# An fp32 transformer stack on one core: the attention mixer's value panels, the order of its head steps, and its output rows

## The chip, the cores and the metric
One Trainium2 chip, one of its cores. The metric is the device time of one execution in microseconds (us), as the median of several runs. Three runs of the kernel before are shown, and one more execution was profiled.

## The reference, cut to what matters
Six layers with 256 tokens and 1024 features run one after the other, all in fp32. Each layer is a feed-forward sublayer, a mixer and a second feed-forward sublayer, each behind an RMS norm and added to the stream. The mixers are HGRN, differential attention, pooling, HGRN again, a hybrid and a recurrent one. The change is in the differential attention (eight heads, each with two groups of 64 query and key features and one value of 128 features):

```python
def diff_attention(x, w_in, lam, subln_w, w_out, layer):
    ...
    q, k, v = jnp.split(x @ w_in, 3, axis=-1)
    ...
        s = jnp.einsum('bhgqd,bhgkd->bhgqk', qb, k).astype(f32) * scale
        s = s - slopes[None, :, None, None, None] * dist
        p = jax.nn.softmax(jnp.where(allowed, s, -jnp.inf), axis=-1)
        w = p[:, :, 0] - lam_full * p[:, :, 1]
        return jnp.einsum('bhqk,bhkv->bhqv', w.astype(v.dtype), v)
    ...
    o = rmsnorm(o, subln_w) * (1.0 - lam_init)
    return o.reshape(B, S, D_MODEL) @ w_out
```

## The kernel before, in words
Activations lie with features on partitions and the 256 tokens along the free axis. Weights come in panels of 1 MB (1024 rows by 256 columns, `[128, 2048]` in memory), one DMA each from the queue of SyncE, into five slots `raw`. A slot is loaded again once TensorE has done the product of the panel in it (`panel_done`). All panels of the program form one list, and each engine goes through it in order.

**Split panels.** An fp32 product is made of reduced-precision parts. ScalarE copies a panel to its high part `whi` (line 1555) and VectorE subtracts it to get the low part `wlo` (line 1747), four panels ahead of TensorE (`AHEAD`). The input `xs` holds a high and a low half for each of eight feature tiles. `tile_product` issues, for each tile, one matmul of `whi` with 512 columns (line 1980) and one of `wlo` with 256 (line 1981). ScalarE copies the second half of the sum out of PSUM (line 1645, `corr_copied`), VectorE adds it (line 1827, `panel_out`) and multiplies by the input's norm factor (line 1917).

**Whole panels.** Output projections of mixers (`out_rows`, `out_rest`, line 2130) and the value panels of the two HGRN mixers (`token_product`, line 2033) use the raw fp32 weights, without a split. A value panel has the input `y` as its stationary operand (written by `whole_input`, line 1572), so that the result has tokens on partitions; ScalarE alone reads it out (`read_tokens`, line 1579, `tokens_out`), scaled by a norm factor for each token, which needs two small sums (line 2104) and two small operations on ScalarE (lines 1565, 1567).

**The attention mixer** reads twelve panels in the order q0 k0 v0 q1 k1 v1 and so on; a panel holds two heads (a pair). All twelve are split panels. Work of the heads is put between them by the table `AT_DELAYS`: a step of pair j stands behind panel 3j + d on its engine, cut off at 12, so what is due later stands behind the last panel, one step after the other. The engines run these lists strictly in order. For each head: `scores` (line 565, TensorE), `max` (bias, maximum: lines 637, 642 and 645, VectorE), `exp` (line 606, ScalarE), `weights` (lines 650 to 659, VectorE), `turn` (transposes of the weights, line 574, TensorE), `wT` (line 611, ScalarE), `values` (lines 582 to 584, TensorE). For each pair: `turn_values` (line 556, TensorE; its copy out is line 599 on ScalarE), `out` (line 664), `square` (614), `sums` (587), `rstd` (618, 620) and `norm` (669). Only when the step behind panel 12 is over does TensorE begin the output projection: `out_products` takes all eight feature tiles of the mixer's output for the first two panels (lines 2164 and 2165), then `out_rest` the other two. The transposes share PSUM bank 2, values and sums bank 3, the scores banks 0 and 1.

The rows of q, k and weights are double-buffered by pair or by head (`at`). The projection's output panels may begin when the bank of the panel two before has been read (`out_begin`).

Of the kernel before, what the change touches and what calls it, by code (L numbers as in the profile page):

```python
# [12 lines left out]
ACT = mybir.ActivationFunctionType  # L13
AX_X = mybir.AxisListType.X
# [49 lines left out]
def build(nc, a, out):  # L64
# [9 lines left out]
    for l in range(4):  # L74
# [6 lines left out]
        elif l == 1:  # L81
            subs.append(dict(kind=DIFF, gain=g + 2, layer=l, segs=[Segment("diff_in", 3 * D // PC), out_proj("diff_out")]))
# [42 lines left out]
    with ctx:  # L125
# [379 lines left out]
        AT_SUM, AT_REC = 4, 8  # L505

        def at_slot(n):
            return mix[:, 2 + n // 4, 2 * (n % 4):2 * (n % 4) + 2, :]

        def at(name, j):  # L510

            names = ("q", "k", "vt", "w", "wT")
            return at_slot(2 * names.index(name) + j % 2 if name in names else 10 + ("v", "sq", "r").index(name))
# [10 lines left out]
        def at_panel(p):  # L524
            return "qkv"[p % 3], p // 3


        AT_DELAYS = dict(
            pe=(("scores0", 3), ("turn_values", 4), ("scores1", 4), ("turn0", 5), ("turn1", 6), ("values0", 6), ("values1", 7),
                ("sums", 8)),  # L530
            act=(("exp0", 3), ("values", 4), ("exp1", 4), ("wT0", 5), ("wT1", 6), ("square", 7), ("rstd", 8)),
            dve=(("max0", 3), ("weights0", 4), ("max1", 4), ("weights1", 5), ("out", 7), ("norm", 8)))

        def at_steps(engine, p, step):

            left = []
            for j in range(KD // 2):
                for name, d in AT_DELAYS[engine]:
                    if min(3 * j + d, 3 * KD // 2) == p:
                        left.append((3 * j + d, j, name))  # L540
            for _, j, name in sorted(left, key=lambda x: x[:2]):
                step(name, j)

        def pe_at_step(pe, s, groups):
            n0, dg, mm = 0, P // groups, nc.tensor.matmul

            def step(name, j):
                n = n0 + j + 1
                h = int(name[-1]) if name[-1] in "01" else 0
                m = 2 * (n - 1) + h + 1  # L550
                if name == "turn_values":
                    pe.wait_ge(sem("at_values_in"), n)
                    if j:
                        pe.wait_ge(sem("at_wT"), m - 1)
                    for c in range(4):
                        e = nc.tensor.transpose(pm[:, 2, c * P:(c + 1) * P], flat_pair(at("v", j))[:, c * P:(c + 1) * P], ident[:, :])
                    e.then_inc(sem("at_values_turned"), 1)
                elif name.startswith("scores"):
                    pe.wait_ge(sem("at_keys_in"), n)
                    if m > 1:  # L560
                        pe.wait_ge(sem("at_scores_read"), m - 1)
                    for g in range(groups):
# [5 lines left out]
                elif name.startswith("turn"):  # L568
                    pe.wait_ge(sem("at_weights"), m)
                    pe.wait_ge(sem("at_vt"), n if h == 0 else n)  # L570
                    if h:
                        pe.wait_ge(sem("at_wT"), m - 1)
# [3 lines left out]
                elif name.startswith("values"):  # L576
                    pe.wait_ge(sem("at_wT"), m)
                    if j and h == 0:
                        pe.wait_ge(sem("at_rstd"), n - 1)
# [139 lines left out]

# [1556 lines left out]
```

## Time and profile before

| | |
|---|---|
| median of three runs | 3265.2 us (3262.81 to 3276.85) |
| the profiled execution | 3276.81 us, of which the span of its instructions is 3275.1 us |
| mean granted TensorE clock | 0.983 of full speed |
| TensorE busy | 97% of the span |
| VectorE, ScalarE busy | 68%, 52% |
| attention mixer: third panel to the first output row | 753.4 to 865.6 us |
| attention mixer: output projection | 865.6 to 895.6 us |

Each row of the page or of the trace names a source line, an engine, an operation and what it writes and reads. Times are from the start of the span. In brackets stands the idle time of the engine ahead of a row, and what ended it. An end of a matmul is modelled: the next one starts before it, so that what a step costs is read from one start to the next. An fp32 matmul has two records.

### The profile page before, as it was taken

What the parts mean: (1) busy time and instruction counts of PE and PEld (TensorE: products, weight loads), DVE (VectorE), ACT (ScalarE), POOL (GpSimd) and SP (SyncE); (2) the same over time, 40 slices, a digit from 0 to 9 for tenths busy, and PEclk for the clock granted to TensorE, in tenths of its full rate; (3) what the DMA queues carried; (4) which work ended last, traced back from release to release, by engine and by line L of the source; (5) the groups of instructions that cost most, each with busy time, mean ns of one, the idle gap of its engine ahead of it and who ended that gap; (6) DMA issues with size and microseconds to landing.
All of it is one profiled execution on the core that took longest, in us unless ns stands there. A gap on an engine that the chain in (4) does not pass through costs nothing.

```text
span 3275.1 us, 44778 instructions
## 1 busy us (share of the span) xinstructions
PE 3162.5 (97%) x18060; PEld 2734.9 (84%) x18060; DVE 2238.2 (68%) x2722; ACT 1703.6 (52%) x2092; POOL 4.2 (0%) x21
## 2 busy tenths in 40 slices
PE   9999999999799999999999999999787999999998
PEld 7888888887688888888888888888675888888887
DVE  7666775757486776675858586775865675866674
ACT  6465555544364654554546554554342554545553
POOL 0000000000000000000000000000000000000000
PEclk9999999999899999999999999999996999999999
DMA  6543454553245454454554345454330455454353
GB/s 225 191 167 129 154 186 175 185 188 129 90 173 187 172 188 169 152 182 167 193 190 155 125 173 181 180 181 173 141 135 1 145 190 182 179 182 162 145 185 124
DMA packets 75357, 534.79 MB, mean 163 GB/s; under 512 B 8480, under 2 KB 8608, under 8 KB 10784
## 3 DMA queue, kind: packets, MB, share of 16 engines
q1 hardware_dynamic: 75168, 532.07, 45.5%
q8 instruction: 143, 2.34, 0.3%
q14 instruction: 46, 0.38, 0.0%
HBM read 530.99 MB, written 1.05 MB: 162 GB/s over the span
## 4 chain that ended last, share of the span: by engine, by line
PE 89%; DVE 5%; DVEq 2%; ACT 2%; issue 1%; SPq 0%; DMA 0%; ACTq 0%
PE pp L1980 36%; PE pp L1981 18%; PE pm L1980 8%; PE pp L2130 4%; PE pm L1981 4%; PE pp L2003 4%; PE pp L1975 2%; PE pp L1974 2%; PE pp L1976 2%; PE pp L2005 2%; PE pp L2033 2%; DVE wlo L1747 1%; DVEq L405 0%; PE pm L1007 0%; ACT whi L1555 0%
## 5 line engine op out<-in xcount | busy, mean ns | idle before, releaser
L1980 PE MATMUL pp<-xs,whi 128*128 128x512 f32 x4720 | 1681.6, 401 | 6.8 <-DVE tsum L1827 6.5
L1747 DVE TENSOR_TENSOR wlo<-raw,whi 128x2048 fp32r<-128x2048 f32 x469 | 1072.7, 2290 | 420.8 <-ACT whi L1555 420.1
L1981 PE MATMUL pp<-xs,wlo 128*128 128x256 f32 x4720 | 1326.3, 281 | 0.0
L1980 PEld LDWEIGHTS pp<-xs,whi 128*128 128x128 f32 x4720 | 888.4, 188 | 237.3 <-DVE tsum L1827 16.0
L1555 ACT ACTIVATE whi<-raw 128x2048 fp32r<-128x2048 f32 x469 | 894.7, 1911 | 291.5 <-DMA raw<-weights 290.8
L1981 PEld LDWEIGHTS pp<-xs,wlo 128*128 128x128 f32 x4720 | 893.3, 189 | 0.8 <-issue 0.2
L1645 ACT ACTIVATE corr<-pp 128x512 f32<-128x512 f32 x344 | 204.5, 595 | 638.8 <-PE pp L1981 613.7
L1827 DVE TENSOR_TENSOR tsum<-pp,corr 128x512 f32<-128x512 f32 x331 | 228.5, 690 | 277.1 <-ACT corr L1645 276.6
L1980 PE MATMUL pm<-hs,whi 128*128 128x512 f32 x1120 | 400.2, 397 | 0.0
L1981 PE MATMUL pm<-hs,wlo 128*128 128x256 f32 x1120 | 314.7, 281 | 0.0
L1980 PEld LDWEIGHTS pm<-hs,whi 128*128 128x128 f32 x1120 | 210.9, 188 | 47.8
L1981 PEld LDWEIGHTS pm<-hs,wlo 128*128 128x128 f32 x1120 | 210.2, 188 | 0.0
L1980 PE MATMUL pp<-hs,whi 128*128 128x512 f32 x560 | 202.3, 397 | 0.0
L2003 PE MATMUL pp<-xs,whi 128*128 128x512 f32 x576 | 166.2, 400 | 16.2 <-DVE xs L1758 16.2
L1974 PE MATMUL pp<-hs,whi 128*128 128x256 f32 x560 | 159.7, 285 | 0.0
L1976 PE MATMUL pp<-hs,wlo 128*128 128x256 f32 x560 | 157.4, 281 | 0.0
L1981 PE MATMUL pp<-hs,wlo 128*128 128x256 f32 x560 | 157.4, 281 | 0.0
L1975 PE MATMUL pp<-hs,whi 128*128 128x256 f32 x560 | 157.4, 281 | 0.0
L1657 ACT ACTIVATE hs<-hid 128x512 fp32r<-128x512 f32 x132 | 83.7, 634 | 105.9 <-DVE hid L1843 105.9
L1980 PEld LDWEIGHTS pp<-hs,whi 128*128 128x128 f32 x560 | 105.3, 188 | 26.0
L2003 PEld LDWEIGHTS pp<-xs,whi 128*128 128x128 f32 x576 | 95.5, 188 | 33.6 <-issue 22.5
L2130 PE MATMUL pp<-mix,raw 128*128 128x256 f32 x512 | 115.2, 386 | 2.5 <-DVE mix L356 2.5
(355 smaller groups left out, 3072.6 us busy)
## 6 DMA issues: line engine op xcount, KB each, us to landing
raw<-weights SPq DMA_DIRECT2D x503, 1024.0 KB, 4.8
raw<-weights SPq DMA_DIRECT2D x8, 256.0 KB, 6.2
h<-x_by_feature SPq DMA_DIRECT2D x4, 256.0 KB, 6.7
out<-h SPq DMA_DIRECT2D x4, 256.0 KB, 2.5
vec<-vectors SPq DMA_DIRECT2D x1, 264.0 KB, 2.7
lamrow<-diff_lambda SPq DMA_DIRECT2D x1, 128.0 KB, 10.8
skiprow<-ssm_d SPq DMA_DIRECT2D x1, 8.0 KB, 11.4
```

The source lines that it names most:

```text
L1555: nc.scalar.activation(whi[:, slot, :], raw[:, slot, :], ACT.Copy).then_inc(sem("weights_hi"), 1)
L1645: nc.scalar.activation(two(corr[:, half, :]), banks[:, :, T:2 * T], ACT.Copy).then_inc(sem("corr_copied"), 1)
L1657: nc.scalar.activation(hs[:, 2 * j:2 * j + 2, 0:T], two(hid[:, :]), ACT.Copy).then_inc(sem("hidden_hi"), 1)
L1747: v.tensor_tensor(wlo[:, slot, :], raw[:, slot, :], whi[:, slot, :].bitcast(F32), ALU.subtract).then_inc(sem("weights_lo"), 1)
L1827: v.tensor_tensor(to, banks[:, :, 0:T], two(corr[:, half, :]), ALU.add).then_inc(sem("panel_out"), 1)
L1974: mm(bank[:, 0:T], whi[:, slot, c:c + P], x_k[:, 0:T], start=start, stop=False)
L1975: mm(bank[:, 0:T], whi[:, slot, c:c + P], x_k[:, T:2 * T], start=False, stop=False)
L1976: return mm(bank[:, 0:T], wlo[:, slot, c:c + P], x_k[:, 0:T], start=False, stop=stop)
L1980: mm(bank, whi[:, slot, c:c + P], x_k, start=start, stop=False)
L1981: return mm(bank[:, 0:T], wlo[:, slot, c:c + P], x_k[:, 0:T], start=False, stop=stop)
L2003: e = mm(bank, whi[:, slot, c:c + P], xs[:, k, :], start=(k == 0), stop=(k == KD - 1))
L2130: return mm(in_banks[p % 2][:, ft, 0:T], raw[:, g % SLOTS, c:c + P], x[:, k, :], start=start, stop=stop)
```

## The change
The four value panels of the attention mixer become whole fp32 panels with tokens on partitions, as in HGRN. With that, `turn_values` (TensorE), its copy (ScalarE), and the splits and reads of these four panels go, and the mixer takes `whole_input` and the sums for each token. The panels come in a new order, q0 k0 q1 k1 v0 q2 k2 q3 k3 v1 v2 v3. A table written out by hand (`AT_PLAN`) says which step of which head stands behind which panel on each engine: every head's `scores`, `turn` and `values` are about one panel behind the previous head's. Of the value and `wT` tiles there are four buffers now. `sums` of pairs 1 to 3 go to the banks of the scores. `out` of a pair comes before the sums of that pair as before; `values` of pair 1 wait for `rstd` of pair 0, those of pairs 2 and 3 for the previous pair's `out`. The output projection's first two panels are taken feature tile by feature tile, and what is left of the last two pairs stands between those rows.

```diff
-            subs.append(dict(kind=DIFF, ..., segs=[Segment("diff_in", 3 * D // PC), out_proj("diff_out")]))
+            subs.append(dict(kind=DIFF, ..., segs=[Segment("diff_in", 3 * D // PC, tokens=(4, 9, 10, 11)), out_proj("diff_out")]))
...
+        AT_PANELS = [(name[0], int(name[1])) for name in "q0 k0 q1 k1 v0 q2 k2 q3 k3 v1 v2 v3".split()]
+        AT_DEEP = dict(q=2, k=2, w=2, sq=2, r=2, vt=4, wT=4)
...
+        def at_sum_bank(j):
+            return (3, 0, 1, 0)[j]
+        AT_PLAN = dict(
+            pe={3: ["scores0"], 4: ["scores1"], 5: ["turn0", "scores2"], 6: ["turn1", "values0", "scores3"],
+                7: ["turn2", "values1", "scores4"], 8: ["turn3", "scores5"], 9: ["turn4", "sums0", "scores6"],
+                10: ["turn5", "values2", "values3", "scores7"], 11: ["turn6", "values4", "values5", "turn7"]},
+            act={4: ["exp0"], 5: ["wT0", "exp1"], 6: ["wT1", "exp2"], 7: ["wT2", "exp3"], 8: ["wT3", "square0", "exp4"],
+                 9: ["wT4", "rstd0", "exp5"], 10: ["wT5", "exp6", "exp7"], 11: ["wT6", "square1", "wT7"]},
+            dve={3: ["max0"], 4: ["weights0", "max1"], 5: ["weights1", "max2"], 6: ["weights2", "max3"], 7: ["out0", "weights3", "max4"],
+                 8: ["weights4", "max5"], 9: ["weights5", "max6", "norm0"], 10: ["weights6", "out1", "max7", "weights7"],
+                 11: ["out2"]})
...
                 elif name == "values":
+                    pe.wait_ge(sem("at_wT"), n + 1)
+                    pe.wait_ge(sem("tokens_out"), t0 + j + 1)
+                    if n == 2:
+                        pe.wait_ge(sem("at_rstd"), 1)
+                    elif n > 2 and h == 0:
+                        pe.wait_ge(sem("at_out_read"), j)
...
                 elif name == "sums":
+                    pe.wait_ge(sem("at_squares"), n + 1)
+                    if n:
+                        pe.wait_ge(sem("at_scores_read"), KD)
+                    if n == 3:
+                        pe.wait_ge(sem("at_rstd"), 2)
...
                 elif name == "wT":
+                    act.wait_ge(sem("at_turned"), n + 1)
+                    if n >= 4:
+                        act.wait_ge(sem("at_out"), n - 3)
...
         def act_diff(act, s, read_out, split, rstd):
...
+            step("rstd", 1)
+            step("square", 2)
+            step("rstd", 2)
+            step("square", 3)
+            step("rstd", 3)
             read_out(s["segs"][1], s)
...
         def dve_diff(dve, s, read_out, split):
...
+            step("norm", 1)
+            step("out", 3)
+            step("norm", 2)
+            step("norm", 3)
             read_out(s["segs"][1], s)
...
         def pe_diff(pe, s, products, down_products, out_products, first_of, column_sums, keep_clock):
...
-            at_steps("pe", 3 * KD // 2, step)
-            out_products(s, mix[:, 0], lambda k: pe.wait_ge(sem("at_normed"), k // 2 + 1))
...
+            begin(s, 0)
+            begin(s, 1)
+            rows(s, mix[:, 0], (0,), everywhere, range(KD), normed)
+            step("sums", 1)
+            step("values", 6)
+            step("values", 7)
+            rows(s, mix[:, 0], (1,), everywhere, range(KD), normed)
+            step("sums", 2)
+            rows(s, mix[:, 0], (2, 3), everywhere, range(KD), normed)
+            step("sums", 3)
+            rows(s, mix[:, 0], (4, 5), everywhere, range(KD), normed)
+            rows(s, mix[:, 0], (6, 7), ((0, 0), (0, 1)), range(KD), normed)
+            rows(s, mix[:, 0], (6, 7), ((1, 0), (1, 1)), range(KD), normed)
+            rest(s, mix[:, 0])
...
             def out_begin(s, p):
...
-                pe.wait_ge(sem("panel_out"), s["segs"][-1].r0 - 1 + p)
+                last = s["segs"][-2].panels - 2 + p
+                if last in s["segs"][-2].tokens:
+                    pe.wait_ge(sem("tokens_out"), s["segs"][-2].t0 + s["segs"][-2].tokens.index(last) + 1)
+                else:
+                    pe.wait_ge(sem("panel_out"), s["segs"][-1].r0 - 1 + p)
...
-        [panels_at(inputs["diff_w_in"][0], [kind * D + c for c in steps for kind in range(3)]),
+        [panels_at(inputs["diff_w_in"][0], ["qkv".index(name[0]) * D + int(name[1]) * PC
+                                            for name in "q0 k0 q1 k1 v0 q2 k2 q3 k3 v1 v2 v3".split()]),
```

A new `rows` over some tiles is the old `out_rows` with all four outputs ("everywhere") of the first two panels for each tile. `whole_input` copies tiles 1 to 4 while the sublayer opens and tiles 0, 5, 6 and 7 behind the first two panels. On VectorE a value panel is a hook and the split of the panel four ahead, in that order; for any other panel the steps come after the split.

## Rows read from the trace of the kernel before

**Rows 1.** The page: busy time, the two split operations, a read of a split panel, loads.
```profile
PE 3162.5 (97%) x18060; PEld 2734.9 (84%) x18060; DVE 2238.2 (68%) x2722; ACT 1703.6 (52%) x2092; POOL 4.2 (0%) x21
...
L1747 DVE TENSOR_TENSOR wlo<-raw,whi 128x2048 fp32r<-128x2048 f32 x469 | 1072.7, 2290 | 420.8 <-ACT whi L1555 420.1
...
L1555 ACT ACTIVATE whi<-raw 128x2048 fp32r<-128x2048 f32 x469 | 894.7, 1911 | 291.5 <-DMA raw<-weights 290.8
...
L1827 DVE TENSOR_TENSOR tsum<-pp,corr 128x512 f32<-128x512 f32 x331 | 228.5, 690 | 277.1 <-ACT corr L1645 276.6
...
raw<-weights SPq DMA_DIRECT2D x503, 1024.0 KB, 4.8
```

**Rows 2.** TensorE's waits, 753.4 to 866: total us, times, longest us.
```profile
PE pm L574 <- DVE mix L659: 18.1, 6, 7.3
PE pm L587 <- ACT mix L614: 4.2, 2, 2.7
```

**Rows 3.** Busy time by stretch: length, engines, clock, DMA.
```profile
753.40:865.60 112.20, 88.59 (x484) 71.49 (x484) 71.68 (x142) 48.66 (x109) 0.00 (x0) 0.87 0.31 112
...
200.00:345.00 145.00, 144.03 (x854) 124.39 (x853) 102.33 (x171) 91.39 (x154) 0.00 (x0) 1.00 0.39 138
```

**Rows 4.** Timeline of TensorE in the attention mixer: start us, us, operation.
```profile
784.64 0.63 PE L1980 MATMUL pp<-xs,whi 128*128 128x512 f32 x1
...
787.17 0.40 PE L1980 MATMUL pp<-xs,whi 128*128 128x512 f32 x1
...
804.35 0.38 PE L582 MATMUL pm<-mix 128*128 128x128 f32 x2
...
805.01 0.60 PE L556 MATMUL pm<-ident,mix 128*128 128x128 f32 x4
...
805.54 0.93 PE L565 MATMUL pm<-mix 64*128 64x128 f32 x8
...
806.41 0.50 PE L1980 MATMUL pp<-xs,whi 128*128 128x512 f32 x1
...
812.17 1.02 PE L587 MATMUL pm<-mix,ones 128*128 128x512 f32 x2
...
813.02 0.49 PE L574 MATMUL pm<-ident,mix 128*128 128x128 f32 x3
...
820.13 0.55 PE L574 MATMUL pm<-ident,mix 128*128 128x128 f32 x3 [0.96 <-DVE mix L659]
...
820.51 0.39 PE L582 MATMUL pm<-mix 128*128 128x128 f32 x2
...
865.56 25.67 PE L2130 MATMUL pp<-mix,raw 128*128 128x256 f32 x112
...
891.06 0.59 PE L2119 MATMUL pm<-mix,ones 128*128 128x256 f32 x2
```

**Rows 5.** TensorE by stretch: one fp32 value panel, one split panel.
```profile
281.46:288.37 6.91, 6.91 (x35) 1.00 0.32 134
290.48:296.14 5.66, 5.66 (x35) 1.00 0.38 162
```

**Rows 6.** Timeline of ScalarE: read of a value panel (HGRN), scaling of an output panel.
```profile
288.57 0.84 ACT L1579 ACTIVATE mix<-pp,rcol 128x256 f32<-128x256 f32 x2 [4.83 <-PE pp L2033]
...
877.51 0.83 ACT L1626 ACTIVATE mix<-pp,vec 128x256 f32<-128x256 f32 x2
```

**Rows 7.** Timeline of VectorE and ScalarE, a head's steps.
```profile
772.69 1.01 DVE L637 SCALAR_TENSOR_TENSOR mix<-dist,pm 128x256 f32<-128x256 f32 x2
...
775.09 0.40 ACT L606 ACTIVATE mix<-mix 128x128 f32<-128x128 f32 x1 [6.40 <-DVE mix L645]
...
776.86 0.58 ACT L1645 ACTIVATE corr<-pp 128x512 f32<-128x512 f32 x1
...
781.49 0.17 DVE L650 RECIPROCAL mix<-mix 128x4 f32<-128x4 f32 x1
...
783.17 1.01 DVE L637 SCALAR_TENSOR_TENSOR mix<-dist,pm 128x256 f32<-128x256 f32 x2
```

More of the change, by code:

```diff
@@ L81, in build @@
         elif l == 1:
[L82 removed]
+            subs.append(dict(kind=DIFF, gain=g + 2, layer=l, segs=[Segment("diff_in", 3 * D // PC, tokens=(4, 9, 10, 11)), out_proj("diff_out")]))
         else:
@@ L505, in build, with at @@
         AT_SUM, AT_REC = 4, 8
[L507 to L513, printed above, removed]
+        AT_PANELS = [(name[0], int(name[1])) for name in "q0 k0 q1 k1 v0 q2 k2 q3 k3 v1 v2 v3".split()]
+        AT_DEEP = dict(q=2, k=2, w=2, sq=2, r=2, vt=4, wT=4)
+        def at(name, n):
+            n = list(AT_DEEP.values())[:list(AT_DEEP).index(name)] + [n % AT_DEEP[name]]
+            return mix[:, 2 + sum(n) // 4, 2 * (sum(n) % 4):2 * (sum(n) % 4) + 2, :]
         def at_scores(hd):
@@ L522, in flat_pair @@
             return buf.rearrange("p h t -> p (h t)")
[L524 to L562, printed above, removed]
@@ new lines, in at_hook, with hook, pe_at_step, step @@
+        def at_hook(engine, step):
+            def hook(p):
+                for name in AT_PLAN[engine].get(p, []):
+                    step(name[:-1], int(name[-1]))
+            return hook
+        def pe_at_step(pe, s):
+            mm, dg, t0 = nc.tensor.matmul, P // 2, s["segs"][0].t0
+            def step(name, n):
+                j, h = n // 2, n % 2
+                if name == "scores":
+                    pe.wait_ge(sem("at_keys_in"), j + 1)
+                    if n:
+                        pe.wait_ge(sem("at_scores_read"), n)
+                    for g in range(2):
@@ new lines, in step, with act_at_step @@
+                    if n:
+                        pe.wait_ge(sem("at_scores_read"), KD)
+                    if n == 3:
+                        pe.wait_ge(sem("at_rstd"), 2)
+                    mm(pm[:, at_sum_bank(n), :], ones[:, :], flat_pair(at("sq", n)), start=True, stop=True).then_inc(sem("at_sums"), 1)
+            return step
+        def act_at_step(act, scale):
+            def step(name, n):
+                if name == "exp":
+                    act.wait_ge(sem("at_max"), n + 1)
+                    sc = at_scores(n)
@@ L2177, in _ @@
                 else:
-                    last = (out_begin, out_rows, out_rest) if s["kind"] in (POOL, HGRN) else out_products
+                    last = (out_begin, out_rows, out_rest) if s["kind"] in (POOL, HGRN, DIFF) else out_products
                     PE_MIX[s["kind"]](pe, s, products, down_products, last, first_of, column_sums, keep_clock)
```

131 lines of the change are left out of this document (55 added, 76 removed).

## The prediction
> **What bounds the kernel now.** I read the page first: TensorE is busy 97% of the span, VectorE 68%, ScalarE 52% [rows 1]. Where TensorE never waits, only its own work counts, and what the change can win lies where it does wait. So I read the busy time by stretch next. The attention mixer, from its third panel to the first row of its output projection, takes 112.2 us, of which TensorE is busy 88.6: 23.6 us idle, at a mean granted clock of 0.87. The first HGRN mixer beside it has 1.0 us idle in 145 us, at clock 1.00 [rows 3]. TensorE's waits name the cause: `turn` waits 18.1 us in six places for `weights` of VectorE, `sums` 4.2 us in two places for `square` [rows 2]. The longest is 7.3 us [rows 2]: all panels are done, and nothing is left beside the last head's chain. Idle time costs twice: a matmul of 512 columns behind such a wait takes 0.63 us, 2.5 us later 0.40 again [rows 4]. That is the granted clock at 1.2 and at 2.4 GHz; a mean of 0.87 means that 26% of the stretch, 29 us, ran at the lower level.
>
> Why it waits: in the old order the scores of a head and its transposes have one panel between them, 5.66 us [rows 5]. The chain across the engines is longer: scores 0.87, max 2.4, exp 1.8, weights 1.7 [rows 4, 7], together 6.8 us, and each link stands behind a panel's read and split in its engine's list. Behind the last panel there is no cover at all.
>
> **The change, part by part.** I walk TensorE's new list from the start of the third panel (753.4) to the start of `out_rest`, the first point that is the same in both kernels. Each step costs what lies from one start to the next at full clock.
>
> Before: the rows start at 865.56. Of the 112 records to 891.06 the last 48 belong to `out_rest`; an fp32 record of 256 columns takes 6.91/32 = 0.216 us [rows 4, 5], so `out_rest` starts at 891.06 - 48 x 0.216 = 880.7. The stretch is 127.3 us.
>
> After:
> 1. Six split panels x 5.66 = 34.0; 0.1 for each that follows a small step (0.50 in place of 0.40 for its first product [rows 4, 5]), 0.6.
> 2. Four value panels x 6.91 = 27.6 [rows 5].
> 3. Sums over features for the input norm: 0.3 as before, and four records of one column for the tokens; no row of this mixer has them, the nearest are the three transposes of a turn, 0.38, so between 0 and 0.5; I take 0.4, since they also start alone: 0.7.
> 4. Eight scores x 0.87 = 7.0 (805.54 to 806.41); eight turns x 0.38 = 3.0; eight values x 0.66 = 5.3 (804.35 to 805.01); four sums x 0.85 = 3.4 [rows 4].
> 5. New waits, worked out below: 0.6.
> 6. The rows of two output panels, 64 records x 0.216 = 13.8 (before 15.1, since they started at the lower clock).
>
> Sum: 34.6 + 27.6 + 0.7 + 18.7 + 0.6 + 13.8 = 96.0 us. **The saving is 127.3 - 96.0 = 31.3 us.**
>
> As a check, the old stretch of 112.2: ten split panels 56.6, small steps 18.7, four `turn_values` x 0.53 = 2.1 (805.01 to 805.54 [rows 4]), sums 0.3, together 77.7; with 23.6 idle 101.3. The other 10.9 us are the lower clock and hand-overs, which 17 us of busy time at half speed (8.5 lost) would nearly fill. So the saving is 23.6 + 10.9 + 2.1 + 1.3 at the rows, less 4 x 1.25 = 5.0 for the dearer value panels, 0.4, and 1.2 for new hand-overs and waits.
>
> Here a rule speaks against the change. A value panel in fp32 takes 6.91 us against 5.66 of a split one [rows 5], so 5.0 us for four. The Trainium skill (FP8 and Floating Point Precision, TensorE Precision Notes) says that true fp32 makes four passes through the array; a split panel makes three. By passes alone, at 2.4 GHz, an estimate from that page is 6.8 against 5.1, 6.8 us for four panels, and the saving would be 29.5. The sum keeps the rows, since the split panel's measured 5.66 holds more than its passes.
>
> **Waits in the new order.** I set each engine's new list against the others, in us after 753.4. The tight places:
> - Panel 4 ends at 19.8. ScalarE reads it (0.8 [rows 6]), makes the high part of panel 8 (1.8), does exp of head 0 (1.8): 24.2. VectorE's weights: 25.9. TensorE wants `turn0` at 26.3. Then max of head 1 frees the scores banks at 27.0, and `scores2`, due at 26.7, waits 0.3. VectorE's split of panel 8 is queued behind that wait for exp: it ends at 30.5 and is needed at 43.
> - From panel 5 on, a head's `turn` stands two panels behind its scores, some 14 us for a chain of 6.8. VectorE has 5.4 us of work for each step of at least 7.6 on TensorE (a read and a scaling at 0.69 each [rows 1], weights 1.7, max 2.3). The nearest margin is `turn1`, 0.1 us: its weights, behind the split of panel 8, are done at 33.6 for 33.7.
> - The last head: exp at 75.9, weights at 77.7; `turn7` is due at 77.4 and waits 0.3.
> - Between the rows: `sums1` ends near 80.8, rstd 82.2, norm 83.0, wanted at 84.5 by tile 2; each later pair has a margin of 1 to 2 us, since 1.7 us of rows for each tile cover the 1.3 of rstd and 0.7 of norm.
> - `out_rest` waits until the first output panel is squared and scaled, some 1.5 us on ScalarE: 0.83 for scaling [rows 6] and a square, which I price as VectorE's 0.69 for as many columns [rows 1]; the second panel's last rows, 1.7 us, cover it. That cover was 3.5 us before. If it is gone, 0.3 us.
>
> Costed at nothing: the four fewer splits (1.9 us each on ScalarE, 2.3 on VectorE [rows 1]), the reads of the old value panels, the copy of turned values and the new `whole_input`. They lie on engines with slack. Bounds for what no row shows: the eight or so new hand-overs cost nothing if all fits, or up to a full wait of the old kind at two of them: 7.3 and 2.7 [rows 2], with a lower clock behind, 13 us in all. Nothing can win beyond the 0.6 of waits and 0.6 of hand-overs. The value taken is near nothing, as in HGRN, which has the same kind of list and 1.0 us idle.
>
> The queues: SyncE's loads wait for `panel_done` in order. Output panels 0 to 3 have no split and land early. The next sublayer's second and third panels load after output panels 0 and 1 are done, now 1.7 us apart in place of 3.5; a load lands in 4.8 us [rows 1], both by 105 at worst, while ScalarE needs them near 99 and 104 and TensorE after 115. A wait of ScalarE there, ahead of the closing squares at 106, could cost 0 to 2 us. I take 0.
>
> The profiled execution took 3276.8 us and becomes 3245.5. It stands 11.6 above the median of the runs shown; taken from the median, 3265.2 - 31.3 = **3233.9 us**, 1.0% less.
>
> **The rivals.**
> - *Some waits stay.* The margins of 0.1 to 0.3 us fall the other way, the first heads' turns wait 1 to 3 us, and the clock falls behind them. For it: all these margins hang on VectorE's strict list, where the split of panel 8 sits between two heads. Against it: a miss moves later work by little, and the slack grows from panel 7 on. With 13 us lost the saving is 18: 3247.
> - *No gain that shows.* The old waits come back between the output rows, where each pair goes TensorE, ScalarE, TensorE, ScalarE, VectorE. If the rows cover nothing, four pairs cost about 5 us each, and with the 5 us of the panels 25 us are gone: saving 6, 3259. Against it: the rows run on other pairs' tiles.
> - *Slower.* VectorE and ScalarE cannot keep one head for each panel, so each of eight turns waits for a whole chain: 4.2 us, as much as the two waits of `sums` before [rows 2], plus 2 at the lower clock, 50 us, less the 31 won: slower by 18, 3284. It decides once VectorE's work for a head and a panel is over TensorE's 7.6 us; by the rows it is 5.4, 7.6 only while splits run.
> - *The change doesn't do what it says*: TensorE's waits go, but the time goes to the next sublayer's first panels, landed or split late. All panels ahead are whole, so splits can't be late by more than a load, 4.8 us; saving 26, in the range.
>
> **How the numbers follow.** Forecast (saving 26 to 33) 0.72; some waits stay (saving 17 to 26) 0.15; less than 16 saved, the second rival, 0.09; slower 0.04. About 0.5%, 16 us, is what a measurement of this kernel can tell from no change. So faster 0.87, same 0.09, slower 0.04. Range: low end 3265.2 - 33 = 3232, less 6 for the spread of the medians, 3226. High end: a saving of 15, 3250, which takes in the first rival and 3 us of spread.
>
> **What would show it.** Right: in the mixer TensorE's idle is under 3 us at a clock of 0.99 or more; no row of `turn` waits over 0.5 us; value panels take 6.9 us each; the stretch from third panel to `out_rest` is 96 us; the first feed-forward panels after it start without a wait. Wrong: a wait of `turn` or `scores` of 1 us or more at heads 0 to 2; rows of the projection waiting for `norm`; slices at the lower clock; or `out_rest` waiting for the scaling by over 0.5 us.

## The result and the profile after

| | before | after |
|---|---|---|
| median | 3264.0 us (4 runs, 3253.6 to 3276.9) | 3224.0 us (4 runs, 3222.5 to 3226.7) |
| ratio | | 0.9876, 95% interval 0.984 to 0.9913 |
| profiled execution | 3276.8 us, span 3275.1 | 3224.1 us, span 3222.3 |
| third panel of the mixer to the start of `out_rest` | 127.3 us | 96.8 us |

The kernel is 1.2% faster, 40 us. That is more than the 31 us forecast, and 2 us beyond the low end of the range; the interval of the ratio holds the forecast all the same (31.3 us less is 0.9904). The profiled executions lie still further apart, 52.8 us by their spans. Two places account for them, the mixer and the feed-forward sublayers. Of the kernel after, one later execution took 7952.4 us where its others took 3222 to 3238; nothing on record says why, and the times below leave it out.

The page of the kernel after, the parts that answer to [rows 1] (lines of source have moved by 5 to 8):

```profile
PE 3133.9 (97%) x18048; PEld 2728.6 (85%) x18048; DVE 2222.6 (69%) x2710; ACT 1701.9 (53%) x2098; POOL 4.5 (0%) x21
...
L1985 PE MATMUL pp<-xs,whi 128*128 128x512 f32 x4656 | 1633.7, 395 | 5.3 <-DVE tsum L1835 4.9
L1755 DVE TENSOR_TENSOR wlo<-raw,whi 128x2048 fp32r<-128x2048 f32 x465 | 1063.4, 2289 | 412.4 <-ACT whi L1563 411.8
```

TensorE's busy time fell by 28.6 us. The mixer's stretch gives 7.3 of them (103.7 busy before, 96.4 after), the lower clock included. The rest is the first sign of a second cause. The splits are four fewer (465 for 469), each as long as before.

TensorE's waits in the mixer, 745 to 866 us, in us in all, times and longest (answers to [rows 2]):

```profile
PE pp L2008 <- DVE xs L1766: 1.0, 1, 1.0
PE pm L555 <- DVE mix L624: 0.3, 1, 0.3
PE pm L563 <- DVE mix L644: 0.2, 1, 0.2
```

The first stands ahead of the sublayer's first panels. Behind the third panel 22.3 us of waits have become 0.5: one of `scores2` (line 555) and one of `turn7` (line 563).

Busy time by stretch, in the columns of [rows 3]: the mixer from its third panel to `out_rest`, and two of its value panels with their hand-overs:

```profile
749.88:846.71 96.83, 96.40 (x535) 80.36 (x535) 58.07 (x131) 46.18 (x118) 0.00 (x0) 1.00 0.37 131
...
763.12:770.23 7.11, 7.11 (x35) 6.00 (x33) 6.92 (x8) 1.86 (x2) 0.00 (x0) 1.00 0.41 147
...
809.95:816.96 7.01, 7.01 (x34) 6.14 (x33) 3.90 (x13) 2.39 (x9) 0.00 (x0) 1.00 0.33 134
```

Idle time is 0.43 us, and the clock is 1.00 where it was 0.87 up to the first output row: all of the stretch ran at 2.4 GHz.

The timeline of TensorE there, at the two waits and in the output rows:

```profile
776.85 0.49 PE L563 MATMUL pm<-ident,mix 128*128 128x128 f32 x3
777.62 0.93 PE L555 MATMUL pm<-mix 64*128 64x128 f32 x8 [0.27 <-DVE mix L624]
778.48 0.50 PE L1985 MATMUL pp<-xs,whi 128*128 128x512 f32 x1
...
828.58 0.55 PE L563 MATMUL pm<-ident,mix 128*128 128x128 f32 x3 [0.15 <-DVE mix L644]
828.96 1.89 PE L2135 MATMUL pp<-mix,raw 128*128 128x256 f32 x8
830.69 1.02 PE L583 MATMUL pm<-mix,ones 128*128 128x512 f32 x2
...
832.89 1.89 PE L2135 MATMUL pp<-mix,raw 128*128 128x256 f32 x8
834.62 1.02 PE L583 MATMUL pm<-mix,ones 128*128 128x512 f32 x2
835.48 3.62 PE L2135 MATMUL pp<-mix,raw 128*128 128x256 f32 x16
838.93 1.02 PE L583 MATMUL pm<-mix,ones 128*128 128x512 f32 x2
839.79 17.45 PE L2135 MATMUL pp<-mix,raw 128*128 128x256 f32 x80
857.08 0.59 PE L2124 MATMUL pm<-mix,ones 128*128 128x256 f32 x2
```

No row of the projection waits. Rows and `sums` follow each other with no idle time from 828.96 on. `out_rest` has the last 48 of the 80 records, so it starts at 857.08 - 48 x 0.216 = 846.7, and 846.7 - 749.9 = 96.8.

**The other 22 us.** The interval of the whole mixer sublayer went from 157.6 to 127.1 us, 30.4 less. What is left of the 52.8, 22.4 us, lies in the feed-forward sublayers, which the change does not touch; what the other mixers gave and took cancels within half a microsecond. One of them (the one behind this mixer), before and then after, in the same columns:

```profile
896.12:1088.40 192.28, 191.21 (x1119) 167.18 (x1118) 134.78 (x135) 102.83 (x109) 0.00 (x0) 1.00 0.51 181
```

```profile
862.14:1052.33 190.19, 189.20 (x1120) 166.90 (x1119) 134.67 (x135) 103.12 (x109) 0.00 (x0) 1.00 0.52 183
...
352.67:544.89 192.22, 191.22 (x1119) 167.20 (x1118) 134.77 (x135) 102.96 (x109) 0.00 (x0) 1.00 0.51 181
```

With as many instructions and the same clock of 1.00, it is 2.1 us shorter. The last line is another feed-forward sublayer of the kernel after, the one behind the first HGRN mixer: it kept the old length. The groups of TensorE in an input projection (562 to about 675 us) show where, before and after (the first window is the longer one); columns are busy us, mean ns, and idle us:

```profile
L1980 PE MATMUL pp<-xs,whi 128*128 128x512 f32 x319 | 113.0, 399 | 0.0
```

```profile
L1985 PE MATMUL pp<-xs,whi 128*128 128x512 f32 x311 | 108.1, 392 | 0.0
```

The 512-column matmul takes 392 ns or 399. From start to start, a pair of matmuls of a split panel (512 columns of `whi`, 256 of `wlo`) follows the last at 0.3467 us or at 0.3533. From its third panel on, an input projection of a feed-forward sublayer has 320 pairs, 320 x 0.0066 = 2.1 us. There are 12 such projections, and I count in each profile how many ran at the short spacing: none before, 11 after. Eleven times 2.1 is 23 us, what the mixer leaves over.

### The profile page after: what moved, and what is told of

It is laid out like the page before. It is cut to its first block, busy times and chain, and to the rows that moved or that the text cites. A ratio compares the mean times of both kernels' runs of the same rounds, so it can differ in the third digit from the quotient of the medians.

```text
span 3222.3 us, 44753 instructions
## 1 busy us (share of the span) xinstructions
PE 3133.9 (97%) x18048; PEld 2728.6 (85%) x18048; DVE 2222.6 (69%) x2710; ACT 1701.9 (53%) x2098; POOL 4.5 (0%) x21
## 4 chain that ended last, share of the span: by engine, by line
PE 92%; DVE 4%; DVEq 2%; ACT 1%; issue 1%; POOL 0%; POOLq 0%; ACTq 0%
PE pp L1985 36%; PE pp L1986 18%; PE pm L1985 8%; PE pp L2135 4%; PE pm L1986 4%; PE pp L2008 4%; PE pp L2038 2%; PE pp L1980 2%; PE pp L1979 2%; PE pp L1981 2%; PE pp L2010 2%; DVEq L405 0%; PE pm L1015 0%; PE pm L1028 0%; PE pp L372 0%
## 5 line engine op out<-in xcount | busy, mean ns | idle before, releaser
L1985 PE MATMUL pp<-xs,whi 128*128 128x512 f32 x4656 | 1633.7, 395 | 5.3 <-DVE tsum L1835 4.9
L1986 PE MATMUL pp<-xs,wlo 128*128 128x256 f32 x4656 | 1304.0, 280 | 0.0
L1985 PEld LDWEIGHTS pp<-xs,whi 128*128 128x128 f32 x4656 | 872.8, 187 | 211.9 <-DVE tsum L1835 14.3
L1986 PEld LDWEIGHTS pp<-xs,wlo 128*128 128x128 f32 x4656 | 880.3, 189 | 0.8 <-issue 0.2
L1985 PEld LDWEIGHTS pm<-hs,whi 128*128 128x128 f32 x1120 | 210.9, 188 | 47.8
L2008 PE MATMUL pp<-xs,whi 128*128 128x512 f32 x576 | 166.2, 400 | 16.8 <-DVE xs L1766 16.8
L2008 PEld LDWEIGHTS pp<-xs,whi 128*128 128x128 f32 x576 | 95.7, 189 | 34.3 <-issue 22.9
```

Of the source, the lines that this page charges most:

```text
L1985: mm(bank, whi[:, slot, c:c + P], x_k, start=start, stop=False)
L1986: return mm(bank[:, 0:T], wlo[:, slot, c:c + P], x_k[:, 0:T], start=False, stop=stop)
L2008: e = mm(bank, whi[:, slot, c:c + P], xs[:, k, :], start=(k == 0), stop=(k == KD - 1))
```

## The experiments

There were two questions: what of the change gives the 30 us in the mixer, and whether the other part belongs to the change at all. The kernels ran in four groups, each beside the kernel before on the same chip. That one's median was 3256.6, 3266.8, 3264.1 and 3271.6 us in the four, so times of different groups compare by their ratios only. "The stretch" is always third panel to `out_rest`, read as above.

### Both kernels again

Neither has an edit.

> The kernel before, unchanged. In its first profile the pairs of matmuls of a split panel (512 and 256 columns) followed each other at 0.354 us in every feed-forward sublayer; in the changed kernel's profile at 0.347 us in the input projections of ten of the eleven that start from a pause. Theory 1 (the level belongs to the execution, not to the kernel): this profile has some feed-forward projections at 0.347, each worth 2.1 us, and the times spread over 3253 to 3277 us. Theory 2 (it belongs to the program): all are at 0.354 again and the times stay at 3265 to 3277 us. Either way the attention mixer takes 127.3 us from its third panel to the start of out_rest.

> The changed kernel, unchanged. Theory 1: the number of projections at 0.347 us differs from the first profile, and the times spread over 3222 to 3245 us. Theory 2: ten of them are at 0.347 again, and all times are within 3222 to 3227 us. Either way the attention mixer takes 96.8 us from its third panel to the start of out_rest.

The kernel before took 3255.6 us (ratio to its own runs 0.9998, 0.9989 to 1.0007), with the stretch at 127.0 and 11 of 12 input projections at the short spacing, where the first profile of the same program had none. The kernel after took 3230.2 us (0.9913, 0.9898 to 0.9929), stretch 96.9, with only 3 of 12 at the short spacing. So the mixer's 30 us repeat to 0.4 us in this pair, and the spacing belongs to the execution, not to the kernel. The profiled executions of the first comparison happened to show the old kernel at its slow end and the new one at its fast end. That the medians lay apart for the same reason is likely but not shown, since one execution of each has a trace.

### The output rows alone, and all but the rows

`rows_alone` is the kernel before with its old panels and table, and only the projection's rows put between the last steps:

```diff
-            at_steps("pe", 3 * KD // 2, step)
-            out_products(s, mix[:, 0], ...)
+            begin(s, 0)
+            begin(s, 1)
+            # at_steps, with rows of tiles 0, 1 ahead of turn1 of pair 2,
+            # of tile 2 ahead of sums of pair 2, of tile 3 ahead of turn1 of pair 3
+            rows(s, mix[:, 0], (4, 5), everywhere, range(KD), normed)
+            rows(s, mix[:, 0], (6, 7), ((0, 0), (0, 1)), range(KD), normed)
+            rows(s, mix[:, 0], (6, 7), ((1, 0), (1, 1)), range(KD), normed)
+            rest(s, mix[:, 0])
```

> The kernel before with only the output rows moved: tiles 0 and 1 stand ahead of turn1 of pair 2, tile 2 ahead of the sums of pair 2, tile 3 ahead of turn1 of pair 3, the rest behind. They fill 6.9 us of waits that were 4.15, 2.73 and 7.26 us. My theory (the rows are a small part, the new order of the head steps is the large one): the stretch from third panel to out_rest falls by 6.9 us and 1 to 3 us of lower clock, to 118 to 120 us. Rival (the rows are what brings the gain): it falls to near 105.

It took 3246.2 us (0.9967, 0.9953 to 0.998); the stretch is 116.4, 10.9 less than before and 1.6 below the expected range. TensorE's waits, 745 to 880 us:

```profile
PE pm L574 <- DVE mix L659: 13.9, 5, 5.6
PE pm L587 <- ACT mix L614: 2.3, 2, 1.4
PE pm L565 <- DVE mix L637: 1.3, 1, 1.3
PE pp L2149 <- DVE tsum L1846: 1.2, 1, 1.2
```

Then its stretch, and the same of the kernel before beside it (`before_again`):

```profile
747.26:863.68 116.42, 97.80 (x547) 79.91 (x547) 72.38 (x143) 52.66 (x116) 0.00 (x0) 0.96 0.30 109
```

```profile
747.07:874.11 127.04, 103.25 (x546) 84.34 (x547) 72.90 (x144) 54.41 (x116) 0.00 (x0) 0.88 0.30 106
```

Half of the gain over `before_again` is idle time (23.8 to 18.6 us), half the clock that comes with it: 0.96 for 0.88, and 5.5 us less of busy time for as many records. Most of the waits for `weights` stay, since they lie among the panels.

`rows_last` is the kernel after with the rows taken out from between the steps:

```diff
-            rows(s, mix[:, 0], (0,), everywhere, range(KD), normed)
             step("sums", 1)
             step("values", 6)
             step("values", 7)
-            rows(s, mix[:, 0], (1,), everywhere, range(KD), normed)
             step("sums", 2)
-            rows(s, mix[:, 0], (2, 3), everywhere, range(KD), normed)
             step("sums", 3)
-            rows(s, mix[:, 0], (4, 5), everywhere, range(KD), normed)
+            rows(s, mix[:, 0], range(6), everywhere, range(KD), normed)
```

> The changed kernel with all output rows behind the last head step, so that the last sums, squares and norms have nothing beside them. My theory: 3 us of waits come back at the sums of pairs 2 and 3, with perhaps 1 us at the lower clock, and the stretch is 99.5 to 101 us in place of 96.8. Rival: without the rows most of the gain goes, and the stretch is over 110.

It took 3230.9 us (0.9919, 0.9903 to 0.9934), stretch 100.2, 3.3 more than after. Rows as cover are worth 10.9 us in the old order, but only 3.3 in the new one. What is left of the gain belongs to the order of the head steps and the value panels together; the next runs take these apart in part.

### The distance between scores and turn

`turns_near` leaves all of the change but puts each `turn` but the last one panel nearer to its scores (`turn7` stood one panel behind `scores7` already):

```diff
-            pe={3: ["scores0"], 4: ["scores1"], 5: ["turn0", "scores2"], 6: ["turn1", "values0", "scores3"],
+            pe={3: ["scores0"], 4: ["scores1", "turn0"], 5: ["scores2", "turn1"], 6: ["values0", "scores3", "turn2"],
...
-                10: ["turn5", "values2", "values3", "scores7"], 11: ["turn6", "values4", "values5", "turn7"]},
+                10: ["values2", "values3", "scores7", "turn6"], 11: ["values4", "values5", "turn7"]},
```

> The changed kernel with every turn one panel earlier on TensorE, so that one panel and not two lies between a head's scores and its transposes, as in the kernel before. All other lists, the fp32 value panels and the output rows stay. My theory (the distance is what removes the waits): turns wait 3 to 5 us at seven heads, some 27 us of idle, and the clock falls behind them for another 5 to 10; the stretch from third panel to out_rest is 128 to 136 us in place of 96.8, no better than before. Rival (the gain is from the work taken off ScalarE and VectorE with the value panels): the waits are half of that, and the stretch stays under 112 us.

It took 3278.2 us (1.0038, 1.0022 to 1.0054): slower than the kernel before. Its waits (750 to 900) and its stretch:

```profile
PE pm L563 <- DVE mix L644: 27.0, 7, 5.4
```

```profile
748.32:889.46 141.14, 114.03 (x534) 94.20 (x535) 58.42 (x131) 45.70 (x118) 0.00 (x0) 0.84 0.25 90
```

The wait came out as expected, 27 us; the stretch is 5 us beyond the expected range, since the lower clock cost more than the 5 to 10 us expected. The same work (534 records here, 535 there) is busy for 114.0 us in place of 96.4: 17.6 us of lower clock, granted 0.84, on top of 27 us idle. So the stretch grew by 44.3 us for 26.7 us more of idle time, 1.7 times as much. One panel of distance decides more than the whole gain.

### The value panels

`values_split` is the kernel after with its four value panels split again, `spread` and `vt` being the old `turn_values` and its copy:

```diff
-    segs=[Segment("diff_in", 3 * D // PC, tokens=(4, 9, 10, 11)), out_proj("diff_out")]
+    segs=[Segment("diff_in", 3 * D // PC), out_proj("diff_out")]
...
-                10: ["turn5", "values2", "values3", "scores7"], 11: ["turn6", "values4", "values5", "turn7"]},
+                10: ["spread1", "scores7", "turn5", "values2", "values3"], 11: ["spread2"]},
...
+            step("turn", 6)
...
+            step("spread", 3)
+            step("values", 4)
+            step("values", 5)
```

> The changed kernel with its new order, its distances and its output rows, but with the value panels split again: four transposes of each pair's values on TensorE, a copy on ScalarE, four splits and four reads more on VectorE. TensorE's own work falls by 4 x 1.25 + 0.4 and rises by 4 x 0.53. My theory (the value panels bring nothing by themselves here and cost TensorE 3.3 us): the stretch is 93.5 to 96 us in place of 96.8. Rival (they are needed, since the engines that split and read them would make TensorE wait): the stretch is over 100 us.

It took 3248.5 us (0.9949, 0.993 to 0.9967), stretch 112.5, 15.6 more than after, where my theory had it no longer at all. Waits, 745 to 865:

```profile
PE pp L2154 <- DVE mix L666: 5.1, 3, 2.6
PE pm L572 <- ACT mix L600: 4.4, 2, 2.6
PE pm L555 <- DVE mix L636: 1.7, 1, 1.7
PE pp L2154 <- DVE tsum L1852: 1.0, 1, 1.0
```

With split panels, values come later: read by two engines, turned by TensorE, copied by ScalarE. So the last steps crowd behind panel 12. `turn` waits for the copy (line 572), and the rows for `norm` (line 2154). But the experiment changes two things, engine work and order. The next one separates them.

`extra_splits` is the kernel after in which ScalarE and VectorE also make the high and low parts of the four value panels, which nothing reads, and the product waits for them:

```diff
+                if g in loaded_anyway:
+                    act.wait_ge(sem(f"raw_landed_{g % SLOTS}"), landings(g))
+                    nc.scalar.activation(whi[:, g % SLOTS, :], raw[:, g % SLOTS, :], ACT.Copy).then_inc(sem("extra_hi"), 1)
...
+                if g in loaded_anyway:
+                    dve.wait_ge(sem("extra_hi"), loaded_anyway.index(g) + 1)
+                    v.tensor_tensor(flat2(mix[:, 7]), raw[:, g % SLOTS, :], whi[:, g % SLOTS, :].bitcast(F32), ALU.subtract
+                                    ).then_inc(sem("extra_lo"), 1)
...
+                if g in loaded_anyway:
+                    pe.wait_ge(sem("extra_lo"), loaded_anyway.index(g) + 1)
```

> The changed kernel, whose fp32 value panels are split all the same: ScalarE makes the high part, VectorE the low part into a tile that nobody reads, at their places four panels ahead, and the value product waits for it. Nothing else of the split form comes back (no transposes, no copy of turned values, no read by VectorE). values_split took 112.5 us from third panel to out_rest, against my 93.5 to 96. My theory now: the four splits cost 3 to 5 us (scores1 some 1.9, turn1 1.0, scores5 and turn3 under 1 each), so 100 to 102 us; the rest of values_split's waits are those for the copies and for the last values. Rival: the splits themselves fill the lists, and the stretch is over 107 us.

It took 3234.5 us (0.9914, 0.9896 to 0.9931), stretch 100.6, 3.7 more than after. The waits, 745 to 865:

```profile
PE pm L557 <- DVE mix L626: 2.5, 2, 2.0
PE pm L565 <- DVE mix L646: 0.9, 1, 0.9
```

The splits cost 3.7 us, since they push `max` and `weights` back. The other 11.9 of the 15.6 us of `values_split` stand beside later values, the order I gave them, and a clock of 0.94 in its stretch, which here stays at 1.00; no run takes these apart. A better order for split value panels was not tried, so how much of these 11.9 us is inherent stays open.

### The spacing of the matmul pairs

If the spacing is a state that a run of equal matmuls falls into, an unlike matmul in the run may set it. `broken_runs` is the kernel after with one 256-column matmul, whose result nothing reads, ahead of every panel of the input projections from the fourth on:

```diff
                     bank_free(seg, p)
+                    if p > 2:
+                        mm(pm[:, 2, 0:T], ones[:, :], keep[:, :], start=True, stop=True)
                     panel_product(...)
```

> The changed kernel with one more matmul of ones (256 columns, fp32, 0.43 us) ahead of each panel from the fourth on in all twelve feed-forward input projections. It asks what holds the spacing of 0.347 or 0.354 us through a whole projection. Theory A (the level is drawn again at each break in the row of pairs): the panels of one projection are at both levels, and no projection is wholly at one. Theory B (the level is fixed for a stretch by how TensorE resumed from its last wait): each projection is at one level throughout, as without the breaks. Either way 19 x 0.43 = 8.2 us more for each projection, some 98 us in all.

> The changed kernel once more. With theory 1 of the first two runs (the level belongs to the execution) its times lie between 3222 and 3245 us, and the kernel before on this chip is 28 to 34 us slower by the median, the 30.4 us of the mixer and a remainder of a few projections.

It took 3323.7 us (1.0172, 1.0149 to 1.0195), with the feed-forward interval at 198.4 for 190.2: the 19 added matmuls of each cost 0.43 us apiece, as expected. All 12 projections ran at the short spacing. The unchanged kernel on the same chip (3235.9 us; 0.9902, 0.9887 to 0.9918) had 4 of 12. So the break sets the spacing but costs more than it brings. Hence one break for each projection, `break_once` with `if p == 3:` in the place of `if p > 2:`, and `break_small`, which has `if p > 2:` with one column in place of 256.

> The changed kernel with one matmul of ones (256 columns, fp32) ahead of the fourth panel of each of the twelve feed-forward input projections, 0.43 us each. In broken_runs, with nineteen of these in each, all twelve projections ran at 0.347 us for a pair. Theory A (such a break leaves TensorE at the faster spacing): one is enough, all twelve are at 0.347, and the time is 12 x 0.43 = 5 us more and 2.1 less for each projection that is slow in the changed kernel, so 5 us faster than it where five are slow. Theory B (the level comes from how TensorE resumed, and twelve of twelve was the execution's): some projections are at 0.354, and the time is 5 us longer.

> The same with a matmul of one column, ahead of each panel from the fourth on. Theory A: all twelve projections at 0.347, the breaks cost at most 0.1 us each (23 us) and the slow projections' 2.1 us are won back. Theory B: some projections are wholly at 0.354. Theory A2 (a break draws the level anew): both levels within one projection.

> The changed kernel once more, for comparison on the same chip. Theory 1 holds if some of its projections are at 0.354 and the number differs from the profiles before (two, nine and seven of twelve).

Where a text here speaks of two, nine and seven slow projections in the profiles of the kernel after, that was read from a few panels; by the mean spacing over whole projections it is one, nine and eight.

`break_once` took 3227.5 us (0.9882, 0.9866 to 0.9899), the unchanged kernel beside it 3233.0 us (0.9901, 0.9885 to 0.9917): 5.5 us faster, as expected, though the two intervals overlap. `break_small` took 3284.1 us (1.0062, 1.005 to 1.0075). Groups of one input projection (561 to 670 us) in `break_once`, then four panels of one in `break_small`, each from its break to the next:

```profile
L1985 PE MATMUL pp<-xs,whi 128*128 128x512 f32 x312 | 108.6, 392 | 0.0
...
L2074 PE MATMUL pm<-keep,ones 128*128 128x256 f32 x2 | 0.6, 378 | 0.0
```

```profile
602.94:608.81 5.87, 5.87 (x36) 5.13 (x35) 4.88 (x5) 3.04 (x3) 0.00 (x0) 1.00 0.51 181
608.81:614.59 5.78, 5.78 (x37) 5.08 (x35) 3.68 (x4) 2.92 (x3) 0.00 (x0) 1.00 0.56 181
614.59:620.46 5.87, 5.87 (x37) 5.13 (x35) 4.88 (x5) 3.04 (x3) 0.00 (x0) 1.00 0.51 179
620.46:626.24 5.78, 5.78 (x37) 5.09 (x36) 3.68 (x4) 2.92 (x3) 0.00 (x0) 1.00 0.49 181
```

One break of 256 columns holds all 12 projections at the short spacing (feed-forward interval 190.6). Breaks of one column leave a mean of 0.3496 us in all twelve, but no panel runs at that mean: the panels alternate, 0.3466, 0.3527, 0.3466 and so on. At the break ahead of the fourth panel the level changed in 10 of 12 projections, at the 216 later breaks every time. Both levels within one projection is what theory A2 had expected; the strict alternation it had not. The sublayer takes 5.3 us more than one at the short spacing (195.4 for 190.1): some 0.9 of it is the ten panels or so at the longer spacing, the rest about 0.23 us for each break, over twice what theory A allowed.

### Both kernels with the spacing held

If the spacing is all that the first comparison held beside the mixer, both kernels with the same break must differ by the mixer alone. `before_break` is the kernel before with the edit of `break_once`; `break_half` is `break_once` with 128 columns.

> The kernel before with the break of break_once (one matmul of ones ahead of the fourth panel of each feed-forward input projection). Theory A (the break pins the spacing at 0.347 us): all twelve projections fast, times within 3 us of each other but for one or two, and the median 30.4 us above break_once_again, near 3257 us, since only the mixer is left to differ. Rival (the spacing stays a matter of the execution, or something else outside the mixer differs too): a spread of 10 us or more, or a difference under 26 or over 35 us.

> The changed kernel with the break, once more, on this chip. Theory A: twelve of twelve at 0.347 us, median 3224 to 3229 us.

> The same with a break of 128 columns, half as long. If any fp32 matmul between two pairs pins the spacing: twelve of twelve at 0.347 and 2 to 3 us less than break_once_again, 3222 to 3226 us. If its length matters (the one-column break left a mean of 0.350 and cost 5.3 us for each projection): some projections above 0.347.

`before_break` took 3254.5 us (3251.0 to 3260.8; ratio 0.9952, 0.9938 to 0.9967) and `break_once_again` 3224.2 (3218.0 to 3230.5; 0.9861, 0.9845 to 0.9878), both with 12 of 12 projections at the short spacing. The difference is **30.3 us**, for 30.4 expected. That it comes out so near is in part luck: each ratio is known to some 5 us, and the profiled stretches of the two differ by 28.6 us (125.5 and 96.9).

That the times of each would lie within 3 us of each other failed: they spread over 10 and 13 us. What else varies is the granted clock. Each execution has its mean clock on record. In `before_break` the three near 3251 us have 0.984 or 0.985, the three at 3257 to 3261 us have 0.981 or 0.982; in `break_once_again` 3218.0 us stands beside 0.991 and 3230.5 beside 0.986. The profiles show one place where: from the start of the hybrid sublayer to its next group of `keep` matmuls (line 2117; such a group opens each sublayer too), `break_once` and then `break_once_again`, one and the same program:

```profile
2227.96:2493.12 265.16, 217.41 (x1097) 174.73 (x1096) 180.66 (x345) 101.68 (x149) 0.00 (x0) 0.86 0.27 96
```

```profile
2226.73:2484.66 257.93, 209.72 (x1097) 169.37 (x1096) 180.15 (x345) 101.68 (x149) 0.00 (x0) 0.89 0.28 98
```

TensorE idles 47.8 and 48.2 us there; the same 1097 records are busy for 7.7 us more at a mean clock of 0.86 than at 0.89. Why an execution is granted less there is open.

`break_half` took 3225.7 us (0.9858, 0.9842 to 0.9873) with 10 of 12 at the short spacing, the other two at 0.353. That reads as if the shorter break did nearly the same, but the panel ahead of it says otherwise. The level of a projection can be read already in the third panel, behind the sums over features that stand in its middle. In the eleven profiles of kernels without a break all 132 projections keep that level to their end. In `break_half` all twelve turn it over: ten were at the longer spacing and became short, the other two were short and became long. One of those two, starts on both sides of the break:

```profile
25.67 0.40 PE L1985 MATMUL pp<-xs,whi 128*128 128x512 f32 x1
...
27.75 0.40 PE L1985 MATMUL pp<-xs,whi 128*128 128x512 f32 x1
...
28.10 0.38 PE L2074 MATMUL pm<-keep,ones 128*128 128x128 f32 x2
...
28.67 0.40 PE L1985 MATMUL pp<-xs,whi 128*128 128x512 f32 x1
...
33.97 0.40 PE L1985 MATMUL pp<-xs,whi 128*128 128x512 f32 x1
```

Six pairs in 2.08 us are 0.3467 each; fifteen in 5.30 us are 0.3533. The break of 256 columns is another case: of the 36 projections with one such break, 28 were at the longer spacing ahead of it and 8 at the short one, and all 36 were short behind it.

Input projections at the short spacing, of 12, in each profile. The medians are of four chips, so that those of different rows do not compare directly:

| kernel | short | stretch, us | median, us |
|---|---|---|---|
| before; before_again | 0; 11 | 127.3; 127.0 | 3264.0; 3255.6 |
| after; after_again; after_third; after_fourth | 11; 3; 4; 6 | 96.8; 96.9; 96.9; 96.9 | 3224.0; 3230.2; 3235.9; 3233.0 |
| rows_alone; rows_last | 7; 11 | 116.4; 100.2 | 3246.2; 3230.9 |
| turns_near; values_split; extra_splits | 6; 7; 8 | 141.1; 112.5; 100.6 | 3278.2; 3248.5; 3234.5 |
| before_break; break_once; break_once_again | 12; 12; 12 | 125.5; 96.9; 96.9 | 3254.5; 3227.5; 3224.2 |

By the ratios (0.9882 and 0.9861) the changed kernel with one break of 256 columns in each input projection is the best version, level with the one of 128 columns (0.9858); its lead of 5.5 us over the changed kernel on the same chip is not clear of noise.

## Why the prediction was right, and where it was wrong

**The direction, the mechanism and the size of the mixer's gain were right.** Step by step:

- *The stretch*, 127.3 to 96.0, came out at 96.8, and at 96.9 three times more.
- *Value panels at 6.91 each*: 7.01 from one start to the next for three of them, 7.11 for the first, against 5.66 still for a split panel (778.48 to 784.14), so 28.1 us for four where I had 27.6. The Trainium skill's rule that was weighed there (FP8 and Floating Point Precision, TensorE Precision Notes: four passes in true fp32) would put the two kinds 1.7 us apart, an estimate from passes alone at 2.4 GHz; the trace has 1.35, nearer to the 1.25 of the rows.
- *New waits of 0.6* (`scores2` 0.3, `turn7` 0.3): 0.27 and 0.15, at these two places and no other. The rows between the steps never waited, `out_rest` did not wait for the scaling, and the next sublayer's first panels had only the wait of 1.0 us for `xs` that they had before.
- *The 0.8 us missing*: 0.5 of it are those hand-overs at the value panels, a term that the sum took at nothing; the rest I did not place.
- *The first three rivals* did not come. The mechanism of "slower" is real, though: `turns_near` waits 27 us in seven places. What decides is the distance of a `turn` from its scores, not VectorE's load, and the change has that distance at two panels for all heads but the last.

**The step that failed** is the low end of the range: "3265.2 - 33 = 3232, less 6 for the spread of the medians". It took all work outside the mixer as the same in both kernels, with 6 us for chance. The runs showed that 12 projections outside the change take 2.1 us more or less each from one execution to the next, 25 us in all, and that with these held the granted clock still spreads one kernel's times over 10 to 13 us. For the profiled execution the forecast was 3245.5 us and the measured time 3224.1: its eleven short projections are 23 us. The three runs shown of the kernel before had a spread of 14 us, and that was the hint: a median of three can lie half of that off, and the median of the kernel after off the other way. The profile of before could have shown it too. All its feed-forward projections are at 0.3533, but the first HGRN mixer has split panels at the short spacing; in this one 13 pairs take 4.51 us from start to start, 0.3469 each:

```profile
234.17 0.40 PE L1980 MATMUL pp<-xs,whi 128*128 128x512 f32 x1
...
238.68 0.39 PE L1980 MATMUL pp<-xs,whi 128*128 128x512 f32 x1
```

I read [rows 3] and [rows 5] for one split panel at full clock and took 5.66 for all, without asking whether all panels of that shape take as long. With the spacing held the difference is 30.3 us, for the 31.3 forecast; in the three later comparisons of the unchanged kernels the ratio is 0.9913, 0.9902 and 0.9901, where 31.3 us are 0.9904. So the mechanism and the size stood, and that the first median fell outside the range was chance that the range had not allowed for.

**A belief that fell** beside it: that the splits taken off the value panels save nothing, being on engines with slack, so that split value panels would have been as fast or faster. At the place they have, they cost 3.7 us, because in a strict list a split between two heads delays the chain behind it. The engine has slack; the list has not.

## What to carry to other kernels

When engines run strict lists, set each step's due time against the whole chain that feeds it, queued work included: here one panel of distance between scores and turn was worth 44 us, more than the whole change brings. Work used as cover pays only where a wait is left: the same output rows gave 10.9 us in the old order and 3.3 in the new. Before giving a range, find out how far the untouched part of the kernel moves between executions, by comparing equal stretches within a profile and across runs; a median of three is no fixed point.

## What the runs showed of the hardware

- At a granted clock of 1.00, the same stream of matmul pairs (512 columns of one reduced-precision operand, 256 of the other) runs at 0.3467 us for each pair or at 0.3533, 1.9% apart. Without a break the level that stands behind the sums of the third panel is kept for the other 19 panels, in 132 of 132 projections, and is drawn anew in the next projection: 0 and 11 of 12 short in two executions of one program.
- A single fp32 matmul of 256 columns between the third and the fourth panel left the short spacing in 36 of 36 projections (`break_once`, `break_once_again`, `before_break`), whichever level stood ahead of it (28 long, 8 short). One of 128 columns turned the level over in 12 of 12. One of a single column ahead of each panel turned it over in 10 of 12 at the fourth panel and in 216 of 216 at the later ones. Why is not known from these runs.
- In the output projections of the feed-forward sublayers the pairs with 512 columns follow at 0.353 in all the profiles.
- Idle time of TensorE cost 1.7 times its length in `turns_near`: 27.1 us idle, and 17.6 us more of busy time for the same work at a mean clock of 0.84.
- One program's executions had a mean granted clock of 0.986 to 0.991 and took 3230.5 to 3218.0 us (`break_once_again`).
